# Gated delta net: the triangular inverse as two diagonal blocks of 64 per head, and sample attention with both groups in one item

## The chip, the core and the metric

One NeuronCore of one Trainium2 chip runs the whole program in one launch. The metric is device time in microseconds (us) of that launch; lower is better.

## What is computed

One decoder layer is evaluated for 1024 prompt rows and for 64 sample rows (8 sequences of 8 new tokens, each with a cache of 256). The layer reads one projection of the normalised input and runs three groups of heads on it (attention, gated delta net, S5), joins them in an output projection, and ends with an MLP. Two parts matter here. The delta net, cut from the reference:

```python
kb = kc * bc[..., None]
a_mat = jnp.where(strict, jnp.einsum('nbhid,nbhjd->nbhij', kb, kc) * decay, 0.0)
rhs = jnp.concatenate([vc * bc[..., None], kb * jnp.exp(gc)[..., None]], axis=-1)
sol = lax.linalg.triangular_solve(a_mat + eye, rhs, left_side=True, lower=True)
u, w = sol[..., :dv], sol[..., dv:]
def step(S, xs):
    v_new = u_i - jnp.einsum('bhck,bhkv->bhcv', w_i, S)
    o_i = (jnp.einsum('bhck,bhkv->bhcv', q_i * jnp.exp(g_i)[..., None], S)
           + jnp.einsum('bhij,bhjv->bhiv', aqk_i, v_new))
    S = (S * jnp.exp(g_last)[..., None, None] + ...)
```

And the sample rows' attention: three softmax branches (keys pooled in blocks of 64, the selected keys, a window), each over a sequence's cache and its own 8 new rows, added with gates `gt[..., 0:1] * o_c + gt[..., 1:2] * o_s + gt[..., 2:3] * o_w`. There are 8 query heads in 2 groups of 4; a group shares its keys and values.

## The kernel before

The stages run one after the other, each with its own instruction streams for the five engines (PE is TensorE, DVE VectorE, ACT ScalarE, POOL GpSimd, SP the DMA queue). Semaphores set the order between engines, and each engine runs its own list in order. The delta net stands between about 406 and 738 us of the span, sample attention between 738 and 821.

**Delta net.** The prompt is cut into 8 chunks of 128 rows (the reference's chunk of 64 is a choice; the result is the same), the sample rows are a ninth chunk of 64 (`TS`). `pairs()` takes them as (0,1), (2,3), (4,5), (6,7), (8). For each of four heads of a chunk the inverse T of the triangular matrix I + A is built by doubling, in `LEVELS` = 7 levels s = 0 to 6 (3 for the ninth chunk): at level s blocks of 2^s rows are joined to blocks of 2^(s+1). `AT` is A transposed, `TT` is T transposed. One level, for one chunk and four heads:

- POOL (L1253) masks: B = AT times the level's mask.
- PE (L1552) multiplies B by T (at level 0 by the identity); 4 matmuls of 128x128.
- ACT (L1321) copies the product out of PSUM to U.
- PE (L1562, L1563) multiplies T by U and U by TT; 8 matmuls (4 at the last level, which needs TT alone).
- DVE (L1408, L1410) subtracts both from T and TT.

Every matmul in float32 is two passes of PE, each with its weight load (PEld), so a 128x128 level of a pair of chunks is 48 passes. The two chunks of a pair alternate, so that one computes while the other's product is copied and subtracted.

Between the levels `after_level` puts steps that prepare the next pair's chunks, one step per level: first chunk a (levels 0 to 3), then chunk b (levels 4 to 6, its last step behind the first chunk's state update). Step 0 is `rows_of` (L1494: 6 transposes), whose result goes through ACT (squares), DVE and POOL (norm by a power, L1224; scaled keys and queries, L1230 and L1231) before step 1 can `turn` it (L1505: 8 transposes). Steps 2 and 3 make the matrices of the next A.

Behind level 6 stands the pair's tail: for each chunk the products with T (L1571, copied by ACT at L1327; L1613), the new values (copied by ACT at L1333), the output and the update of the state S.

**Sample attention.** Four items: two halves of four sequences, times the two groups. Scores of an item: for each of its four sequences five matmuls (L2177 to L2181: selected cache and new keys, window cache and new keys, pooled keys) with 64 rows and 32 weight columns. DVE adds the distances (L2298), reduces and scales (L2302 to L2317), ACT takes exponentials; PE turns the probabilities (L2190 to L2193: 7 transposes) and multiplies them by the values (L2205 to L2213: 19 matmuls, 64 weight columns). Items 0 to 3 have all their scores before the first turn.

## Time and profile before

| | us |
|---|---|
| median of 3 runs | 2117.62 (2117.27 to 2118.31) |
| profiled execution, its own time | 2112.89 |
| its span in the trace | 2110.7 |
| PE busy in the span | 1911.5 (91%) |
| DVE busy | 898.9 (43%) |
| ACT busy | 546.1 (26%) |
| POOL busy | 259.0 (12%) |

The page's shares are means over the whole span; most of PE's time is the output projection and the MLP. The two stages that the change touches take 416 of the 2110.7 us, so they are read by themselves, by stretches of the span. PEclk in such a view is the clock granted to TensorE, as a share of the full one.

### The profile page before, as it was taken

The numbers are of one execution on the slowest core, as the hardware profiler recorded it, in microseconds if no ns is written. First come the engines' busy times: TensorE is split into PE (matmuls) and PEld (weight loads), VectorE is DVE, ScalarE is ACT, GpSimd is POOL, SyncE is SP. The second block draws the span as 40 slices with busy tenths as digits, with TensorE's granted clock in tenths as the row PEclk, the third lists the DMA queues.
The fourth block names the chain that finished last, engine by engine and source line by source line (L and its number), as shares of the span: only waits on it lengthen the run. The fifth ranks groups of instructions, "written<-read, shape, count | busy, mean of one in ns | idle before, by whom it ended". The sixth has DMA issues, their size and how long they took to land. (4 is left out here: it accounts for less than half of the span.)

```text
span 2110.7 us, 26308 instructions
## 1 busy us (share of the span) xinstructions
PE 1911.5 (91%) x10850; PEld 1624.8 (77%) x10850; DVE 898.9 (43%) x1580; ACT 546.1 (26%) x994; POOL 259.0 (12%) x291
## 2 busy tenths in 40 slices
PE   2899989769998697999999898899999999999997
PEld 2898889768888575555555587899999999999996
DVE  4643351134444523454444353244444444444446
ACT  3122221212222114444443332211111211111212
POOL 0200000043344101000110000100000011111000
PEclk6899999879999665899999999999999999999999
DMA  4000022110000010000000301111111111111102
GB/s 117 22 31 22 23 72 104 54 56 1 1 1 26 12 59 25 1 1 1 20 21 0 125 1 40 41 40 60 40 41 41 41 60 41 41 41 41 41 30 85
DMA packets 31161, 80.03 MB, mean 38 GB/s; under 512 B 11183, under 2 KB 17279, under 8 KB 25763
## 3 DMA queue, kind: packets, MB, share of 16 engines
q1 hardware_dynamic: 30978, 78.27, 11.0%
q8 instruction: 86, 1.41, 0.3%
q14 instruction: 33, 0.26, 0.0%
q0 software_dynamic: 64, 0.09, 0.0%
HBM read 70.32 MB, written 10.12 MB: 38 GB/s over the span
## 5 line engine op out<-in xcount | busy, mean ns | idle before, releaser
L275 PE MATMUL ps<-mix_hi,wbuf 128*128 128x364 f32 (+1 forms) x768 | 254.1, 331 | 9.5 <-DVE wbuf L2659 6.1
L276 PE MATMUL ps<-mix_lo,wbuf 128*128 128x364 f32 (+1 forms) x768 | 253.6, 330 | 0.0
L277 PE MATMUL ps<-mix_hi,wbuf 128*128 128x364 f32 (+1 forms) x768 | 253.6, 330 | 0.0
L2695 DVE TENSOR_TENSOR x<-x,ps 128x512 f32<-128x512 f32 (+1 forms) x288 | 190.7, 684 | 120.2 <-PE ps L277 120.2
L275 PE MATMUL ps<-wbuf,mlp_hid_hi 128*128 128x512 f32 x576 | 225.3, 391 | 4.4 <-DVE wbuf L2659 4.4
L276 PE MATMUL ps<-wbuf,mlp_hid_hi 128*128 128x512 f32 x576 | 225.2, 391 | 0.0
L277 PE MATMUL ps<-wbuf,mlp_hid_lo 128*128 128x512 f32 x576 | 225.0, 391 | 0.0
L2681 DVE TENSOR_TENSOR mlp_hid_lo<-mlp_rect,mlp_hid_hi 128x364 fp32r<-128x364 f32 (+1 forms) x96 | 75.1, 783 | 290.0 <-ACT mlp_hid_hi L2602 290.0
L2653 POOL TENSOR_TENSOR mlp_rect<-mlp_rect 128x364 f32<-128x364 f32 (+1 forms) x96 | 76.0, 791 | 661.3 <-ACT mlp_rect L2624 661.3
L275 PEld LDWEIGHTS ps<-mix_hi,wbuf 128*128 128x128 f32 x768 | 146.3, 190 | 10.5 <-DVE wbuf L2659 6.4
L276 PEld LDWEIGHTS ps<-mix_lo,wbuf 128*128 128x128 f32 x768 | 145.8, 190 | 0.5
L277 PEld LDWEIGHTS ps<-mix_hi,wbuf 128*128 128x128 f32 x768 | 145.7, 190 | 0.0
L1893 PE MATMUL ps<-tokens,pa_vaug 128*65 128x512 f32 x264 | 141.3, 618 | 0.0
L1977 ACT ACTIVATE tokens<-ps 128x512 f32<-128x512 f32 (+1 forms) x148 | 88.0, 595 | 184.9 <-PE ps L1872 96.9
L275 PEld LDWEIGHTS ps<-wbuf,mlp_hid_hi 128*128 128x128 f32 x576 | 108.7, 189 | 27.0 <-DVE wbuf L2659 4.8
L277 PEld LDWEIGHTS ps<-wbuf,mlp_hid_lo 128*128 128x128 f32 x576 | 108.7, 189 | 22.7
L276 PEld LDWEIGHTS ps<-wbuf,mlp_hid_hi 128*128 128x128 f32 x576 | 108.7, 189 | 22.2
L2047 DVE TENSOR_REDUCE pa_mxp<-ps 128x1 f32<-128x512 f32 (+4 forms) x154 | 91.1, 617 | 75.2 <-PE ps L1847 49.2
L2624 ACT ACTIVATE mlp_rect<-ps 128x364 f32<-128x364 f32 (+1 forms) x96 | 45.4, 473 | 299.0 <-PE ps L277 299.0
L2596 ACT ACTIVATE wbuf<-mlp_raw_down 128x2048 fp32r<-128x2048 f32 x16 | 30.6, 1913 | 315.1 <-PE ps L277 315.1
L1841 PE MATMUL ps<-pa_Ka,pa_Q 128*128 128x512 f32 (+3 forms) x192 | 88.2, 520 | 21.9 <-DVE pa_part L2040 20.3
L1253 POOL TENSOR_TENSOR dn_B<-dn_AT,dn_level 128x512 f32<-128x512 f32 (+1 forms) x59 | 73.5, 1262 | 127.8 <-DVE dn_aqkT L1388 47.9
(532 smaller groups left out, 3724.2 us busy)
## 6 DMA issues: line engine op xcount, KB each, us to landing
out_raw<-in_w_up SPq DMA_DIRECT2D x16, 1024.0 KB, 4.8
mlp_raw_down<-in_w_down SPq DMA_DIRECT2D x16, 1024.0 KB, 4.8
feat_raw<-in_w_feat SPq DMA_DIRECT2D x12, 512.0 KB, 4.5
spare<-in_w_token SPq DMA_DIRECT2D x4, 1056.0 KB, 6.0
ln_x<-in_x_prompt SPq DMA_DIRECT2D x8, 512.0 KB, 4.1
ck<-in_cache_nsa SPq DMA_DIRECT2D x16, 256.0 KB, 3.0
out_raw<-in_w_out SPq DMA_DIRECT2D x4, 1024.0 KB, 4.7
x<-in_x_prompt SPq DMA_DIRECT2D x8, 512.0 KB, 6.2
```

The lines of the kernel that those rows point to most:

```text
L275: pe.matmul(out, lhs[0], rhs[0], start=first, stop=False)
L276: pe.matmul(out, lhs[0], rhs[1], start=False, stop=False)
L277: return pe.matmul(out, lhs[1], rhs[0], start=False, stop=last)
L1253: pool.tensor_tensor(B[:n, x, :, :n], AT[:n, k % 4, :, :n], mask, ALU.mult).then_inc(b_ready, 1)
L1841: last = pe.matmul(bank[:, x * w:(x + 1) * w], Q0[:, g, h * P:(h + 1) * P], Ka[:, br, g, k0:k0 + w], start=x == 0, **args)
L1893: pe.matmul(m.ps[:VW, 5 + br, :], v, PT[st % PTN][:k, :], start=first, stop=s == branch_end(n, br)).then_inc(pv_step, 1)
L1977: act.activation(PT[st % PTN][:rows, :], m.ps[:rows, 3 + x % 2, :], ACT.Exp).then_inc(ring_out, 1)
L2047: dve.tensor_reduce(mxp[:, heads[0]:heads[-1] + 1, col:col + 1], bank[:, 0:w * len(heads)].rearrange("p (h n) -> p h n", h=len(heads)), AX ...
L2624: act.activation(rect[:, (rank[u] - 1) % RT, :w], m.ps[:, u % 8, :w], ACT.Relu).then_inc(rectified, 1)
L2653: pool.tensor_tensor(part, part, part, ALU.mult).then_inc(squared, 1)
L2681: dve.tensor_tensor(hid[1][:, g % 2, a, o:o + w], rect[:, (rank[u] - 1) % RT, :w], hid[0][:, g % 2, a, o:o + w], ALU.subtract).then_inc(hi ...
L2695: dve.tensor_tensor(part, part, m.ps[:n, u % 8, :], ALU.add).then_inc(added, 1)
```

## The change

In the delta net the 64x64 diagonal blocks of T and TT are kept and doubled by themselves up to level 5 (`in_blocks`), with 64x64 matmuls that alternate between the upper and the lower half of the rows; `own` and `beside` are the two halves of columns of the same buffers, in which T and TT, or B's working part and the kept blocks of AT, lie side by side. ACT copies these blocks of AT out once per chunk (`at_kept`), and POOL's masks are 64 columns wide. Level 6 joins the blocks: it takes the corner of AT by itself, with no mask, and writes one corner of TT. DVE subtracts T and TT in one instruction. The other steps of a pair, and where they stand, are as before.

In sample attention an item is two sequences with both groups: `qS` holds a query's columns with zeros in the other group's rows, so a matmul runs over all 128 rows with 64 weight columns, and each sequence's own 8 new keys and 4 pooled keys lie behind its cache in `kT`. The values are multiplied with both groups' 128 weight columns at once, and half of the result is used. Eight small DMAs move the new values to where a matmul can read them. Each DVE step covers two branches in one instruction.

```diff
...
-    t["level"] = np.concatenate([((i >> s) == (p >> s) + 1) & (i >> (s + 1) == p >> (s + 1))
-                                 for s in range(LEVELS)], 1).astype(f)
+    ph, ih = p % 64, np.arange(64)[None, :]
+    t["level"] = np.concatenate([((ih >> s) == (ph >> s) + 1) & (ih >> (s + 1) == ph >> (s + 1))
+                                 for s in range(LEVELS - 1)], 1).astype(f)
+    t["eye64"] = (ph == ih).astype(f)
...
+        def in_blocks(k):
+
+            return SLEVELS if k == TS else LEVELS - 1
+
+        def order_b(k, s):
+
...
+        def blocks(k):
+
+            return [slice(0, BW)] + [slice(BW, P)] * (k < TS)
+
+        def own(t, k):
+            return t[:ROWS[k], k % 2, :, 0:BW]
+
+        def beside(t, k):
...
+                pool.memset(TT[:], 0.0).then_inc(s_zero, 1)
...
@@ -1241,16 +1255,19 @@
                 for p, pair in enumerate(pairs()):
                     for s in range(levels(pair[0])):
                         for k in pair:
+                            if s == in_blocks(k):
+                                continue
                             n, x = ROWS[k], k % 2
-                            pool.wait_ge(a_ready, 4 * (k + 1))
+                            if s == 0:
+                                pool.wait_ge(at_kept, k + 1)
                             if s:
                                 pool.wait_ge(bt, order(k, s - 1))
                             elif k >= 2:
                                 pool.wait_ge(bt, order(k - 2, LEVELS - 1))
                             if s == 1:
                                 pool.wait_ge(t_ready, order(k, 0))
-                            mask = C["level"][:n, s * P:s * P + n].unsqueeze(1).to_broadcast([n, H, n])
-                            pool.tensor_tensor(B[:n, x, :, :n], AT[:n, k % 4, :, :n], mask, ALU.mult).then_inc(b_ready, 1)
+                            mask = C["level"][:n, s * BW:s * BW + BW].unsqueeze(1).to_broadcast([n, H, BW])
+                            pool.tensor_tensor(own(B, k), beside(B, k), mask, ALU.mult).then_inc(b_ready, 1)
                         after_level(p, s, {1: scale})
...
@@ -1310,15 +1327,22 @@
                 for p, pair in enumerate(pairs()):
                     for s in range(levels(pair[0])):
                         for k in pair:
+                            n, x = ROWS[k], k % 2
                             if s == 0:
+                                act.wait_ge(a_ready, 4 * (k + 1))
+                                if k >= 2:
+                                    act.wait_ge(b_ready, order_b(k - 2, in_blocks(k - 2) - 1))
+                                for blk in blocks(k):
+                                    last = act.activation(B[blk, x, :, BW:P], AT[blk, k % 4, :, blk], ACT.Copy)
+                                last.then_inc(at_kept, 1)
                                 continue
-                            n, x = ROWS[k], k % 2
                             act.wait_ge(bt, order(k, s))
                             if s > 1:
                                 act.wait_ge(tut, order1(k, s - 1))
                             elif k >= 2:
...
-                            act.activation(U[:n, x, :, :n], heads(m.ps[:n, 3 * x, :])[:, :, :n], ACT.Copy).then_inc(u_ready, 1)
+                            rows = slice(0, n) if s < in_blocks(k) else slice(BW, P)
+                            act.activation(U[rows, x, :, 0:BW], heads(m.ps[rows, 3 * x, 0:H * BW]), ACT.Copy).then_inc(u_ready, 1)
...
@@ -1396,19 +1420,27 @@
                         for k in pair:
                             n, x = ROWS[k], k % 2
                             if s == 0:
-                                eye = m.ident[:n, :n].unsqueeze(1).to_broadcast([n, H, n])
-                                dve.wait_ge(b_ready, order(k, 0))
-                                link(dve.tensor_tensor(TT[:n, x, :, :n], eye, B[:n, x, :, :n], ALU.subtract))
+                                eye = C["eye64"][:n].unsqueeze(1).to_broadcast([n, H, BW])
+                                dve.wait_ge(b_ready, order_b(k, 0))
+                                link(dve.tensor_tensor(beside(T, k), eye, own(B, k), ALU.subtract))
                                 dve.wait_ge(bt, order(k, 0))
-                                dve.tensor_tensor(T[:n, x, :, :n], eye, heads(m.ps[:n, 3 * x, :])[:, :, :n],
-                                                  ALU.subtract).then_inc(t_ready, 1)
+                                dve.tensor_tensor(own(T, k), eye, heads(m.ps[:n, 3 * x, 0:H * BW]), ALU.subtract).then_inc(t_ready, 1)
                                 continue
                             dve.wait_ge(tut, order1(k, s))
-                            if s < levels(k) - 1:
-                                link(dve.tensor_tensor(T[:n, x, :, :n], T[:n, x, :, :n],
-                                                       heads(m.ps[:n, 3 * x + 1, :])[:, :, :n], ALU.subtract))
-                            dve.tensor_tensor(TT[:n, x, :, :n], TT[:n, x, :, :n],
-                                              heads(m.ps[:n, 3 * x + 2, :])[:, :, :n], ALU.subtract).then_inc(t_ready, 1)
+                            both = heads(m.ps[:n, 3 * x + 1, :])
+                            if k < 2 and s == in_blocks(k) - 1:
+                                dve.wait_ge(s_zero, 2)
+                            if s < in_blocks(k) - 1:
+                                dve.tensor_tensor(T[:n, x], T[:n, x], both, ALU.subtract).then_inc(t_ready, 1)
+                            elif s < in_blocks(k):
+                                if k < TS:
+                                    dve.tensor_tensor(T[0:BW, x, :, 0:BW], T[0:BW, x, :, 0:BW], both[0:BW, :, 0:BW], ALU.subtract)
+                                for blk in blocks(k):
+                                    last = dve.tensor_tensor(TT[blk, x, :, blk], T[blk, x, :, BW:P], both[blk, :, BW:P], ALU.subtract)
+                                last.then_inc(t_ready, 1)
+                            else:
+                                dve.tensor_scalar(TT[0:BW, x, :, BW:P], heads(m.ps[0:BW, 3 * x + 2, 0:H * BW]), -1.0, None,
+                                                  ALU.mult).then_inc(t_ready, 1)
...
@@ -1539,7 +1571,8 @@
                     for s in range(levels(pair[0])):
                         for k in pair:
                             n, x = ROWS[k], k % 2
-                            pe.wait_ge(b_ready, order(k, s))
+                            if s < in_blocks(k):
+                                pe.wait_ge(b_ready, order_b(k, s))
...
@@ -1549,8 +1582,13 @@
                                 pe.wait_ge(s_ready, k - 1)
                                 pe.wait_ge(w_ready, 2 * (k - 1))
                             for h in range(H):
-                                last = pe.matmul(m.ps[:n, 3 * x, h * P:h * P + n], B[:n, x, h, :n],
-                                                 T[:n, x, h, :n] if s else m.ident[:n, :n], start=True, stop=True)
+                                if s == in_blocks(k):
+                                    last = pe.matmul(m.ps[BW:P, 3 * x, h * BW:(h + 1) * BW], AT[0:BW, k % 4, h, BW:P], T[0:BW, x, h, 0:BW],
+                                                     start=True, stop=True)
+                                    continue
+                                for blk in blocks(k):
+                                    last = pe.matmul(m.ps[blk, 3 * x, h * BW:(h + 1) * BW], B[blk, x, h, 0:BW],
+                                                     T[blk, x, h, 0:BW] if s else m.ident[blk, blk], start=True, stop=True)
                             last.then_inc(bt, 1)
                         for k in pair:
                             if s == 0:
@@ -1558,9 +1596,17 @@
                             n, x = ROWS[k], k % 2
                             pe.wait_ge(u_ready, order1(k, s))
                             for h in range(H):
+                                if s == in_blocks(k):
+                                    last = pe.matmul(m.ps[0:BW, 3 * x + 2, h * BW:(h + 1) * BW], U[BW:P, x, h, 0:BW], TT[BW:P, x, h, BW:P],
+                                                     start=True, stop=True)
+                                    continue
                                 if s < levels(k) - 1:
-                                    pe.matmul(m.ps[:n, 3 * x + 1, h * P:h * P + n], TT[:n, x, h, :n], U[:n, x, h, :n], start=True, stop=True)
-                                last = pe.matmul(m.ps[:n, 3 * x + 2, h * P:h * P + n], U[:n, x, h, :n], TT[:n, x, h, :n], start=True, stop=True)
+                                    for blk in blocks(k):
+                                        pe.matmul(m.ps[blk, 3 * x + 1, h * P:h * P + BW], T[blk, x, h, BW:P], U[blk, x, h, 0:BW],
+                                                  start=True, stop=True)
+                                for blk in blocks(k):
+                                    last = pe.matmul(m.ps[blk, 3 * x + 1, h * P + BW:(h + 1) * P], U[blk, x, h, 0:BW], T[blk, x, h, BW:P],
+                                                     start=True, stop=True)
                             last.then_inc(tut, 1)
...
+                for b in range(NB):
+                    sp.dma_start(vnew[:, b], m.kv[b * NQ:(b + 1) * NQ, TS, VSEL:VSEL + 3 * P].rearrange("q (a n) -> q a n", a=3)[:, ::2, :]
+                                 ).then_inc(rows_moved, 16)
+
+            @block.gpsimd
+            def _(pool):
+                pool.memset(qS[:], 0.0).then_inc(q_zero, 1)
 
...
                 def scores(it):
-                    g, h = items[it]
-                    half = slice(64 * g, 64 * g + 64)
                     if it >= 2:
                         pe.wait_ge(sc_out, it - 1)
-                    sel, win, cmp = score_banks(it)
-                    for b in range(4):
-                        rows = slice(32 * b, 32 * b + 32)
-                        seq = 4 * h + b
-                        q = qS[half, seq].rearrange("p r q -> p (r q)")
-                        pe.matmul(sel[rows, 0:PAST], q, kT[half, 0, seq * PAST:(seq + 1) * PAST], start=True, stop=True)
-                        pe.matmul(sel[rows, PAST:], q, kselT[half, :], start=True, stop=True)
-                        pe.matmul(win[rows, 0:PAST], q, kT[half, 1, seq * PAST:(seq + 1) * PAST], start=True, stop=True)
-                        pe.matmul(win[rows, PAST:], q, kwinT[half, :], start=True, stop=True)
-                        last = pe.matmul(cmp[rows, :], q, kcT[half, :], start=True, stop=True)
+                    x = 2 * (it % 2)
+                    for i in range(2):
+                        rows = slice(64 * i, 64 * i + 64)
+                        b = 2 * it + i
+                        q = qS[:, b].rearrange("p g r q -> p (g r q)")
+                        pe.matmul(m.ps[rows, x, 0:KEYS + BLK], q, kT[:, b, SEL, :], start=True, stop=True)
+                        last = pe.matmul(m.ps[rows, x + 1, 0:KEYS], q, kT[:, b, WIN, 0:KEYS], start=True, stop=True)
                     last.then_inc(sc, 1)
 
                 def turn_probs(it):
@@ -2186,37 +2236,33 @@
                     pe.wait_ge(scaled, it + 1)
...
                 def values(it):
-                    g, h = items[it]
-                    half = slice(64 * g, 64 * g + 64)
                     pt = PT[:, it % 2]
                     pe.wait_ge(p_out, 3 * (it + 1))
                     if it >= 2:
                         pe.wait_ge(o_out, it - 1)
-                    acc = m.ps[half, 4 + it % 2, 0:P]
...
+                            pe.matmul(acc, ck[:, PAGES * b + a, 384:512], pt[:, a, rows], start=a == 0, stop=False)
+                            pe.matmul(acc, cw[:, PAGES * b + a, 128:256], pt[:, 2 + a, rows], start=False, stop=False)
+                        for c in (SEL, WIN):
+                            pe.matmul(acc, vnew[:, b, c, :], pt[:NQ, 4 + c, rows], start=False, stop=False)
+                        last = pe.matmul(acc, vcs[:, b, :], pt[:BLK, 6, rows], start=False, stop=True)
                     last.then_inc(pv, 1)
```

PE's order in the delta net, level 4 of a pair: `dn_B` is the masked matrix, `mixT` the next chunk's columns for `rows_of`, `dn_qk` the first input of `turn`; and the alternation of two lines, which repeats eight times, is shown once. First as it was before:

```order
L1552 MATMUL ps<-dn_T,dn_B 128x128 x8
L1562 MATMUL ps<-dn_U,dn_TT 128x128
L1563 MATMUL ps<-dn_TT,dn_U 128x128
L1494 MATMUL ps<-ident,mixT 128x128 x6
L1552 MATMUL ps<-dn_T,dn_B 128x128 x8
L1562 MATMUL ps<-dn_U,dn_TT 128x128
L1563 MATMUL ps<-dn_TT,dn_U 128x128
L1505 MATMUL ps<-ident,dn_qk 128x128 x4
```

And now, the same place:

```order
L1590 MATMUL ps<-dn_T,dn_B 64x64 x16
L1605 MATMUL ps<-dn_U,dn_T 64x64 x2
L1608 MATMUL ps<-dn_T,dn_U 64x64 x2
L1526 MATMUL ps<-ident,mixT 128x128 x6
L1590 MATMUL ps<-dn_T,dn_B 64x64 x16
L1605 MATMUL ps<-dn_U,dn_T 64x64 x2
L1608 MATMUL ps<-dn_T,dn_U 64x64 x2
L1537 MATMUL ps<-ident,dn_qk 128x128 x4
```

Every product stands where it stood, with twice as many matmuls of a quarter of the size, and the six transposes of `rows_of` and the first of `turn` stand between the same levels.

ACT's order at the end of a pair and the start of the next, before: `dn_wT` and `dn_vnew` belong to the tail of the old pair, `dn_sq` and `dn_qk` to the preparation of a later chunk, `dn_U` to level 1.

```order
L1327 ACTIVATE dn_wT<-ps 64x256 x2
L1333 ACTIVATE dn_vnew<-ps 128x256
L1327 ACTIVATE dn_wT<-ps 64x256 x2
L1333 ACTIVATE dn_vnew<-ps 128x256
L1283 ACTIVATE dn_sq<-ps 128x512
L1284 ACTIVATE dn_qk<-ps 128x512
L1321 ACTIVATE dn_U<-ps 128x512 x2
```

And now:

```order
L1351 ACTIVATE dn_wT<-ps 64x256 x2
L1357 ACTIVATE dn_vnew<-ps 128x256
L1351 ACTIVATE dn_wT<-ps 64x256 x2
L1357 ACTIVATE dn_vnew<-ps 128x256
L1336 ACTIVATE dn_B<-dn_AT 64x4x64 x4
L1300 ACTIVATE dn_sq<-ps 128x512
L1301 ACTIVATE dn_qk<-ps 128x512
L1345 ACTIVATE dn_U<-ps 128x4x64 x2
```

The copies of the kept blocks, four for the two chunks, stand between the last copy of the new values and the squares.

PE's order in sample attention, where the scores begin, before: `cw` is the window cache, turned by 16 transposes ahead of the scores.

```order
L2161 MATMUL ps<-ident,cw 128x128 x16
L2177 MATMUL ps<-sa_kT,sa_qS 32x256
L2178 MATMUL ps<-sa_kselT,sa_qS 32x64
L2179 MATMUL ps<-sa_kT,sa_qS 32x256
L2180 MATMUL ps<-sa_kwinT,sa_qS 32x64
L2181 MATMUL ps<-sa_kcT,sa_qS 32x32
```

And now:

```order
L2216 MATMUL ps<-ident,cw 128x128 x16
L2230 MATMUL ps<-sa_kT,sa_qS 64x268
L2231 MATMUL ps<-sa_kT,sa_qS 64x264
L2230 MATMUL ps<-sa_kT,sa_qS 64x268
L2231 MATMUL ps<-sa_kT,sa_qS 64x264
```

Twenty matmuls of an item became four.

## Rows read from the trace of the kernel before

**Rows 1.** Windows: length; busy us of PE, PEld, DVE, ACT, POOL; clock; DMA; GB/s.

```profile
446.00:692.00 246.00, 220.78 (x1800) 207.12 (x1800) 109.62 (x208) 62.57 (x142) 100.25 (x94) 0.99 0.02 6
692.00:738.00 46.00, 27.93 (x190) 24.14 (x189) 27.29 (x42) 5.03 (x14) 9.94 (x4) 0.65 0.06 13
738.00:822.00 84.00, 78.17 (x538) 60.54 (x539) 18.76 (x74) 17.42 (x63) 0.64 (x3) 0.60 0.12 37
```

**Rows 2.** The same view: levels of the pair of chunks 2 and 3.

```profile
517.28:529.03 11.75, 9.66 (x80) 8.84 (x80) 8.81 (x16) 2.94 (x6) 8.03 (x9) 1.00 0.00 1
529.03:550.67 21.64, 21.57 (x182) 20.89 (x183) 8.75 (x15) 5.21 (x12) 8.67 (x7) 1.00 0.01 1
550.67:559.20 8.53, 6.83 (x58) 6.26 (x56) 5.55 (x11) 3.32 (x7) 5.23 (x7) 1.00 0.01 3
559.20:566.24 7.04, 6.97 (x57) 6.54 (x57) 1.38 (x2) 2.18 (x6) 2.44 (x2) 1.00 0.00 0
566.24:578.40 12.16, 10.37 (x81) 9.41 (x81) 3.66 (x12) 2.43 (x7) 1.26 (x1) 1.00 0.00 1
```

**Rows 3.** Who waited for whom, 446 to 692: total us, times, longest.

```profile
ACT dn_U L1321 <- PE ps L1552: 57.5, 44, 5.2
PEld ps L1552 <- POOL dn_B L1253: 18.5, 22, 1.7
```

**Rows 4.** Timeline of chunk 4's preparation: start, length, engine, operation, count, idle before.

```profile
519.44 0.82 PE L1494 MATMUL ps<-ident,mixT 128*128 128x128 f32 x6
525.99 0.61 POOL L1231 TENSOR_TENSOR dn_qg<-dn_qk,dn_gate 128x256 f32<-128x256 f32 x1
527.29 0.60 PE L1505 MATMUL ps<-ident,dn_qk 128*128 128x128 f32 x4
```

**Rows 5.** Timeline of small tiles on PE and PEld (shapes: weights, then moving).

```profile
137.17 2.16 PE L996 MATMUL ps<-fs_x,mixT 128*64 128x8 f32 x64
152.23 3.71 PE L971 MATMUL ps<-fs_x,mixT 128*64 128x128 f32 x64
692.36 0.54 PEld L1552 LDWEIGHTS ps<-ident,dn_B 64*64 64x64 f32 x8
```

**Rows 6.** Timeline, tail of the first pair, and two rows of the sample chunk.

```profile
504.81 0.38 PE L1514 MATMUL ps<-dn_featT 64*128 64x128 f32 x2
505.12 1.16 PE L1571 MATMUL ps<-dn_TT,dn_kbg 128*128 128x128 f32 x8
506.31 0.78 ACT L1327 ACTIVATE dn_wT<-ps 64x256 f32<-64x256 f32 x2 [1.03 <-PE ps L1571]
694.31 0.71 POOL L1253 TENSOR_TENSOR dn_B<-dn_AT,dn_level 64x256 f32<-64x256 f32 x1 [15.57 <-DVE dn_T L1403]
702.68 1.78 PEld L1571 LDWEIGHTS ps<-dn_TT,dn_kbg 64*128 64x128 f32 x8 [0.69 <-DVE dn_TT L1410]
```

**Rows 7.** TensorE's busy time and granted clock in three stretches.

```profile
506.00:508.00 2.00, 1.13 (x11) 1.00 0.00 0
694.00:696.00 2.00, 0.92 (x8) 0.83 0.18 33
764.00:790.00 26.00, 26.00 (x135) 0.50 0.00 1
```

**Rows 8.** Sample attention: two stretches of PE, and four rows of VectorE.

```profile
761.33:790.52 29.19, 29.19 (x161) 0.54 0.00 1
790.52:820.98 30.46, 27.71 (x182) 0.50 0.00 1
767.61 1.01 DVE L2298 SCALAR_TENSOR_TENSOR sa_probs<-sa_dist,sa_slope,ps 128x320 f32<-128x320 f32 x2 [6.43 <-PE ps L2181]
768.81 0.97 DVE L2302 TENSOR_REDUCE sa_mx<-sa_probs 128x1 f32<-128x320 f32 x3
792.90 0.16 DVE L2310 TENSOR_SCALAR sa_rs<-sa_rs 128x3 f32<-128x3 f32 x1
794.39 0.16 DVE L2310 TENSOR_SCALAR sa_rs<-sa_rs 128x3 f32<-128x3 f32 x1
```

More of the change, by code:

```diff
@@ new lines, in score_banks @@
+            return m.ps[:, x:x + 2, 0:KEYS], m.ps[:, x, KEYS:KEYS + BLK]
+        (consts, weights, cw_loaded, rows_moved, sigmoids, q_zero, q_out, turned, pages_out, window_out, pooled, pool_out, gated, sc, sc_out,
+         nm_ready, exp_done, scaled, p_turned, p_out, pv, o_out, vec) = (sem(n) for n in (
+             "consts", "weights", "cw_loaded", "rows_moved", "sigmoids", "q_zero", "q_out", "turned", "pages_out", "window_out", "pooled",
+             "pool_out", "gated", "sc", "sc_out", "nm_ready", "exp_done", "scaled", "p_turned", "p_out", "pv", "o_out", "vec"))
@@ L2289, in _ @@
-                dve.wait_ge(pool_out, 8)
-                dve.wait_ge(consts, 64)
+                    dve.tensor_copy(kT[:, 2 * a:2 * a + 2, WIN, 0:PAST], m.ps[:, a, :].rearrange("p (b n) -> p b n", b=2)).then_inc(window_out, 1)
+                dve.wait_ge(gated, 1)
+                link(dve.tensor_reduce(gates[:], picked[:].rearrange("p i (h c) -> p i c h", c=3), AX.X, ALU.add))
                 def rows(it):
-                    g, h = items[it]
                     probs = probs_of[:, it]
+                    keys, blocks = score_banks(it)
@@ L2295, in rows @@
                     dve.wait_ge(sc, it + 1)
-                    for b, ((o, w), src) in enumerate(zip(BR, score_banks(it))):
-                        table = dist[:, h, :] if b < 2 else dcmp[:, h, :]
-                        last = dve.scalar_tensor_tensor(probs[:, o:o + w], table, slope[:, g:g + 1], src, ALU.mult, ALU.add)
-                    last.then_inc(sc_out, 1)
+                    dve.scalar_tensor_tensor(two(probs), dist[:, 0:KEYS].unsqueeze(1).to_broadcast([P, 2, KEYS]), slope[:, 0:1], keys,
+                                             ALU.mult, ALU.add)
@@ L2300, in rows @@
+                    dve.scalar_tensor_tensor(branch(probs, CMP), dist[:, KEYS:], slope[:, 0:1], blocks,
+                                             ALU.mult, ALU.add).then_inc(sc_out, 1)
                     dve.wait_ge(sc_out, it + 1)
-                    for b, (o, w) in enumerate(BR):
-                        last = dve.tensor_reduce(mx[:, it, b:b + 1], probs[:, o:o + w], AX.X, ALU.max)
-                    link(last)
+                    dve.tensor_reduce(mx[:, it, 0:2], two(probs), AX.X, ALU.max)
```

183 lines of the change are left out of this document (84 added, 99 removed).

## The prediction

> **What bounds the kernel now.** I read the views by stage first, since the page's shares average over stages. In the paired loop of the delta net (446 to 692) PE is busy 220.8 of 246 us, and the next engine, DVE, 110 [rows 1]: PE is the bound, and its granted clock there is .99, so its passes run at the upper level (2.4 GHz). In the two stretches behind it the clock is .65 and .60 [rows 1]: there PE spends much time at the lower one (1.2 GHz), and a pass costs more.
>
> One pair of chunks, level by level [rows 2]: levels 0 and 1 take 11.75 us, levels 2 to 4 21.64, level 5 8.53, level 6 7.04, the tail 12.16, in all 61.1. Levels 2 to 4 are PE without a gap (21.57 of 21.64 busy, 182 passes, .119 each). Levels 0 and 1, and level 5, are not: PE is busy 9.7 of 11.75 and 6.8 of 8.53. What they wait for shows in the view of waits: PE's loads wait 18.5 us for POOL's masks, 22 times [rows 3]. The longest name there, ACT waiting 57.5 us for PE's products, is an engine with time to spare. POOL's mask is late because the norm of the next chunk stands on POOL: from `rows_of` at 519.44 to the scaled queries, at 525.99 + .61, are 7.16 us, and `turn` (527.29) comes behind it [rows 4]. This chain of ACT, DVE and POOL is a floor for a stretch between `rows_of` and `turn`, whatever PE does.
>
> **The delta net's products.** A level of a pair had 48 passes of 128x128, 5.7 us at .119. It gets 96 of 64x64. No row has such passes on alternating tiles, so I bound them. The ninth chunk's 64x64 passes on one tile took .54 for 8, .067 each [rows 5]: the upper end, nothing overlapping. 64 passes that alternate between two column halves took 2.16, .034 each, and with 128 moving columns 3.71, .058, half of the loop's .119 [rows 5]: two tiles do run beside each other. I take .034, half of .067, as alternating is what the new code does. A level is then 3.3 us instead of 5.7.
>
> - Levels 2 to 4: 288 passes by .034 (9.8), the 38 other passes at .119 (4.5), .4 for waits and changes of tile: 14.7, so -6.9.
> - Levels 0 and 1: `rows_of` ends its wait at +1.25 (32 passes and its start), the chain's 7.16 makes 8.4; POOL's remaining work is 1.15 and its new mask .71 (the ninth chunk's mask had that size [rows 6]): level 2 starts at 10.3 instead of 11.75, -1.45. Without the chain it would be 5.
> - Level 5: chain-bound too, 7.16 less the .7 by which `rows_of` stands ahead, and .95 for eight transposes (.60 for four and overlap [rows 4]): 7.4 for 8.53, -1.1.
> - Level 6: 32 passes on single tiles by .067 (2.1), .7 for a copy that fewer passes cover, 24 others at .119: 5.7 for 7.04, -1.3.
> - Tail: the kept blocks add two ACT copies (.78 for two such sizes [rows 6]) and a POOL mask (.71) between ACT's last copy and level 0. The last products of the tail stand behind that copy as well and hide most: +.3, between 0 and 1.5.
>
> A change of tile size leaves a gap: the last passes with 64 rows begin at 504.81, two in some .2, and the next with 128 rows at 505.12 [rows 6], so about .1 us; it is in the sums. The Trainium skill ("TensorEngine Tiling (Array Packing)", Key Properties) says that a change of the tiling mode drains the engine, which speaks against the change; it gives no price.
>
> Together -10.45 a pair, -41.8 for four; the first pair has no tail to hide its .78 + .71, +1.5. DVE's single subtraction and the narrower masks lie beside PE. The ninth chunk keeps its 64 rows: nothing. **-40.3 at full clock.**
>
> **The clock.** This is the part that I price last and trust least. The clock stayed at full in a tail where PE was busy only 1.13 of 2 us, with tiles of 128 rows [rows 7]. It fell (.83 in the stretch) at 694 to 696, where PE had been on 64x64 tiles and then waited 2.04 us for POOL; and it was .50 through 764 to 790, where PE never idled but worked with 64 rows [rows 7, 8]. So tiles of 64 rows hold the clock less well. The new loop has tiles of 64 rows in each block, two together, and a wait of over 2 us before each of seven `turn`s. At the lower clock a pass of 128 columns goes from .119 to .222 (1.78 for 8 [rows 6]), nearly double. I expect the clock to fall at the waits, and the dense levels, with both halves of the array at work, to bring it back. Where it returns I can't read; I take half a level's extra behind chunk a's `turn` (1.8; a level at half costs 3.3 more), three quarters behind chunk b's (2.5, the small join follows), and a tail entered low costs its 10.37 us of PE [rows 2] almost again: 9.0 by .222/.119, 10.4 doubled, I take 9.7. Four times 1.8, three times 2.5 and two of four tails: 7.2 + 7.5 + 19.4 = **+34.1**, between 0 and far more (below). The delta net comes to -6.2.
>
> **Sample attention.** Scores end the wait at 761.33 and reach the first `turn_probs` at 790.52, 29.2 us of unbroken PE at a clock of .54 [rows 8]. Now an item has 8 passes of 264 or 268 columns with all 128 rows: at .119 for 128 columns .25 each, 2.0 us. DVE's two fused steps on 528 columns instead of 640 (1.01 and .97 [rows 8]: .83 and .8), the pooled keys' .24, the maximum's .17 and starts make 2.3 an item, so DVE is the bound. Three items and the first scaling (792.90 to 794.39, 1.5 [rows 8]) come before the first turn: 761.3 + .4 + 2.0 + 3 x 2.3 + 1.5 = 772.1, 18.4 earlier. Behind it 2.3 + 1.5 = 3.8 to the second turn; three turns of 7 passes (4.7) and 112 passes of values, whose weight loads have 128 columns, at the lower clock's .222 (24.9); .8 for the last copies: 806.3 against 820.98, **-14.7**. I keep the lower clock, which the old stretch had throughout [rows 8]; at the full one it would be up to 12 us less. The eight small DMAs and the copies stand ahead of the wait at 761 and are needed after the turn: nothing; if one were late by its own length, a few us.
>
> **The sum.** -40.3 + 34.1 - 14.7 = -20.9 on the profiled execution's 2112.89 (span 2110.7), 2092.0. That execution lies 4.7 below the runs' median, 2117.62, so the median goes to **2097**. By itself this case runs from 2080 (one tail low) to 2112 (three and a half).
>
> **The rivals.**
> - A, the clock never falls: -40.3 - 14.7 = -55, 2063. For it: the old loop held .99 with pauses. Against it: rows 7. Chance .15.
> - B, all four tails low: another 19.4, 2116, no change to be measured. Chance .13.
> - C, the clock stays low through the loop, slower than before. Levels 0 and 1 +.5; levels 2 to 4 288 x .068 + 38 x .238 + .4 = 29.0, +7.4; level 5 +.6; level 6 +3.7; tail +10: +22 a pair, +89, and +1.5 - 14.7: 2194. It is decided by whether dense levels of alternating 64x64 tiles bring the clock back; if they don't, nothing does. For it 764 to 790, unbroken and low; against it that both halves work here at once. Chance .10.
> - D, the blocks don't overlap, .067 a pass: levels 0 and 1 -.4, levels 2 to 4 24.2 (+2.6), the rest as above: about 0 a pair, then +1.5 - 14.7, 2105 at full clock. The rows of .034 speak against it. Chance .07. The Trainium skill ("TensorE: Matmul & The Clock Gate", Back-to-back issue gap) names about 62 ns per matmul instruction as a floor where hardware decode is off; by it 288 passes would take 17.9 us and the sum at full clock would come to about 2099. The row of .034 disagrees.
>
> The main case has .50, other mixtures .05. **How the numbers follow.** About .2% (4 us) is what a measurement here can tell from no change. Faster: A .15, most of the main case .44, D .06, other .03: .68. Same: parts of B and the main case's upper end: .12. Slower: C .10, B's and the main case's far ends .10: .20. Ends cut to 2 in 10 outside: the low end takes in A, 2060; the high end B with some more clock lost, 2130; C lies outside.
>
> **What would show it.** Levels 2 to 4 near 15 us a pair at clock 1.00 and L1590 to L1608 near .034 a pass: the product step; .067 is D. A stretch of levels 0 and 1 near 10 us: the chain's floor. The clock in the four tails, and in 2 us stretches behind each turn: the +34. A first turn of probabilities some 18 us earlier after the scores' start, and 34 us from there to the end: the sample part. I am wrong if the clock behaves otherwise than a fall at the waits and a return in the dense levels, or if POOL's mask, not PE, ends every level.

## The result and the profile after

The changed kernel takes **2068.94 us** (median of 4 runs, 2065.6 to 2072.31) against 2117.44 beside it: ratio 0.977, 95% interval 0.975 to 0.979, some 48 us less. I forecast 2097, in a range of 2060 to 2130: the sign was right, the size less than half.

The profiled execution (2070.01, span 2068.1) is read first by the same stages as before. A profile shows one execution: in some experiments below (e3, e7, e8, e10) it is 4 to 11 us below the median of its kernel, so what its stretches gain need not be what the median gains. Views of stretches of the changed kernel; columns as in [rows 1]: length, busy us of PE, PEld, DVE, ACT and POOL with their instructions, granted clock, DMA share, GB/s. They are the paired loop, the ninth chunk, the preparation of sample attention (turns of pages and window, pooled keys), the scores up to the first turn of probabilities, and the rest up to the prompt attention.

```profile
461.40:662.10 200.70, 165.44 (x2786) 150.85 (x2786) 77.40 (x183) 54.88 (x150) 62.02 (x83) 0.93 0.03 8
662.10:708.60 46.50, 26.24 (x190) 22.74 (x189) 26.88 (x40) 5.30 (x15) 10.32 (x5) 0.73 0.06 14
708.60:738.20 29.60, 26.43 (x187) 25.82 (x186) 4.95 (x14) 5.46 (x9) 0.14 (x1) 0.62 0.31 90
738.20:747.20 9.00, 5.62 (x32) 3.19 (x32) 6.57 (x23) 4.12 (x18) 0.00 (x0) 0.82 0.01 2
747.20:782.40 35.20, 32.13 (x141) 29.15 (x141) 5.51 (x23) 7.13 (x27) 0.06 (x1) 0.51 0.00 0
```

The same preparation in the kernel before (PE alone, clock, DMA share, GB/s):

```profile
738.70:761.30 22.60, 20.55 (x194) 0.83 0.43 136
```

From starts of instructions that stand in both traces:

| stretch, us | before | changed | difference | forecast |
|---|---|---|---|---|
| first transposes of the delta net to the first pair | 35.6 | 34.6 | -1.0 | +1.5 |
| four pairs | 237.3 | 200.8 | -36.5 | -41.8 + 34.1 |
| ninth chunk, output turns | 46.7 | 46.5 | -.3 | 0 |
| preparation of sample attention | 22.3 | 29.5 | +7.3 | 0 |
| scores to the first turn | 29.2 | 9.1 | -20.1 | -18.4 |
| from there to the prompt attention | 30.8 | 35.1 | +4.4 | +3.7 |
| the rest of the kernel | 1289.4 | 1285.7 | -3.7 | 0 |
| sum | | | -49.9 | -20.9 |

The stretches read here differ by more than the spans (42.6), because what stands ahead of the delta net took 7.3 longer in this execution. It has the same code and still moves from one execution to the next (its end, the first transposes, lies at 419.4 in the profile of before and between 420.9 and 426.7 in those of the changed kernel and the experiments), and the rest of the kernel by some 3 us. So I read each stretch by itself.

Where the loop's time went shows by levels. The pair of chunks 2 and 3 again, beside [rows 2]: levels 0 and 1, 2 to 4, 5, 6, the tail; and below them two stretches of it, behind the first and the second `turn`:

```profile
515.90:526.30 10.40, 6.56 (x143) 1.00 0.01 2
526.30:542.10 15.80, 15.75 (x326) 0.89 0.01 4
542.10:549.20 7.10, 4.21 (x105) 1.00 0.01 2
549.20:557.90 8.70, 8.14 (x59) 0.61 0.00 0
557.90:570.20 12.30, 10.51 (x83) 1.00 0.01 2
526.50:529.90 3.40, 3.40 (x68) 0.52 0.02 7
550.40:557.20 6.80, 6.25 (x35) 0.51 0.00 0
```

Lengths are 10.4, 15.8, 7.1, 8.7 and 12.3; at full clock I had 10.3, 14.7, 7.4, 5.7 and 12.5. The clock falls where I said, behind the waits, for 3.4 us in the first case and 6.8 in the second; levels 2 to 4 and level 6 are 1.1 and 3.0 longer than I had at full clock. The tail is untouched (1.00). Rows of PE in that pair:

```profile
542.12 1.15 PE L1590 MATMUL ps<-dn_T,dn_B 64*64 64x64 f32 x32
543.81 0.28 PE L1608 MATMUL ps<-dn_T,dn_U 64*64 64x64 f32 x4
543.93 0.28 PE L1605 MATMUL ps<-dn_U,dn_T 64*64 64x64 f32 x4
548.25 0.63 PE L1537 MATMUL ps<-ident,dn_qk 128*128 128x128 f32 x4 [2.52 <-issue]
550.95 1.96 PE L1600 MATMUL ps<-dn_TT,dn_U 64*64 64x64 f32 x16 [0.56 <-ACT dn_U L1345]
557.87 1.16 PE L1617 MATMUL ps<-dn_TT,dn_kbg 128*128 128x128 f32 x8
```

32 passes in 1.15 are .036 each, where I took .034. Both figures hold the length of the last pass too; by their starts, four alternating passes come every .12 us (L1608, then L1605), some .03 each. `turn` (L1537) waits 2.52 for the chain; behind it the join's 16 passes (L1600) take 1.96, where 1.14 is the time at full clock (the same passes in e3, below); the tail's first products take the 1.16 that they took before [rows 6].

### The profile page after: what moved, and what is told of

Its sections match the earlier page's. It is cut to its first block and busy times, and to the rows that moved or that the text cites. A ratio compares the mean times of both kernels' runs of the same rounds, so it can differ in the third digit from the quotient of the medians.

```text
span 2068.1 us, 27935 instructions
## 1 busy us (share of the span) xinstructions
PE 1850.6 (89%) x11698; PEld 1576.6 (76%) x11698; DVE 866.3 (42%) x1540; ACT 541.1 (26%) x1001; POOL 223.7 (11%) x285
## 5 line engine op out<-in xcount | busy, mean ns | idle before, releaser
L266 PEld LDWEIGHTS ps<-wbuf,mlp_hid_hi 128*128 128x128 f32 x576 | 108.7, 189 | 26.9 <-DVE wbuf L2703 4.8
L1887 PE MATMUL ps<-pa_Ka,pa_Q 128*128 128x512 f32 (+3 forms) x192 | 88.5, 523 | 22.7 <-DVE pa_part L2086 21.2
L266 PE MATMUL ps<-kvp_whi,h_hi 128*128 128x264 f32 x288 | 82.7, 287 | 5.3 <-DVE kvp_wlo L346 5.3
```

The costliest lines, as they stand in the source:

```text
L266: pe.matmul(out, lhs[0], rhs[0], start=first, stop=False)
L1887: last = pe.matmul(bank[:, x * w:(x + 1) * w], Q0[:, g, h * P:(h + 1) * P], Ka[:, br, g, k0:k0 + w], start=x == 0, **args)
```

## The experiments

**e1 and e2, each half alone.**

```diff
e1, against the changed kernel:
-                        pe.matmul(m.ps[rows, x, 0:KEYS + BLK], q, kT[:, b, SEL, :], start=True, stop=True)
+                        pe.matmul(sel[rows, 0:PAST], q, kT[half, 0, seq * PAST:(seq + 1) * PAST], start=True, stop=True)
...

e2, against the changed kernel:
-                                for blk in blocks(k):
-                                    last = pe.matmul(m.ps[blk, 3 * x, h * BW:(h + 1) * BW], B[blk, x, h, 0:BW],
...
+                                last = pe.matmul(m.ps[:n, 3 * x, h * P:h * P + n], B[:n, x, h, :n],
...
```

> The delta net of the changed kernel with the sample attention of the kernel before. Theory F (the clock falls only for some microseconds behind the turns, and no tail of a pair is run at the lower level): the stretch from the first rows_of to the ninth chunk's first product, 272.9 us before and 235.4 in the changed kernel, is 235 again, and the whole about 37 below before, 2080. Rival P (the prediction's term: the clock takes back 34 of 40): 2111, with tails of pairs at half clock.

> The sample attention of the changed kernel with the delta net of before. In the changed kernel's profile the scores took 20 us less, the values 4 more, and the preparation ahead of the scores (page and window turns, pooled keys) 7.3 more, most of it at the lower clock. Theory F: those 7.3 are where the clock happened to return and not of the change, so the preparation takes about 23 here and the whole is 16 below before, 2101. Rival G: the preparation's new shapes keep the clock low, it takes about 30, and the whole is 9 below, 2109.

Measured: e1 2086.41 (2075.2 to 2087.51; ratio 0.983, 0.980 to 0.986), e2 2100.03 (0.991, 0.990 to 0.993), against 2119.26. In stretches, e1's loop and its preparation (before's code), then e2's preparation (the changed code) and the rest of its sample attention from the first turn:

```profile
456.20:659.10 202.90, 167.10 (x2788) 0.92 0.03 8
705.40:734.90 29.50, 27.43 (x194) 0.61 0.33 104
```

```profile
742.30:765.00 22.70, 19.63 (x186) 0.82 0.41 117
773.10:808.30 35.20, 32.12 (x140) 0.51 0.00 0
```

The delta net's gain is there by itself: 202.9 for the pairs, near the 200.8 above and far from the 230 that my clock term asked for. The preparation is the surprise. Before's code takes 29.5 us behind the new delta net (clock .61), and the changed code 22.7 behind the old one (.82). So rival G is out: the 7.3 us are not of the new shapes. They also explain why e1 lies 6 us above its expected 2080.

**e3, the waits filled.**

```diff
                 def turn(k):
                     n, x = ROWS[k], k % 2
+                    if k > 1:
+                        for _ in range(10):
+                            pe.matmul(m.ps[:, 2, 0:P], m.ident[:], m.ident[:], start=True, stop=True)
                     pe.wait_ge(normed, k + 1)
```

> The changed kernel with ten 128x128 products, whose result nobody reads, on TensorE ahead of each turn of the paired loop, where it waits some 2.5 us for the norm. Theory F (the wait is what lets the clock fall): clock 1.00 through the loop, levels 2 to 4 14.7 instead of 15.8, level 6 5.7 instead of 8.6 where it was low; some 1 us for each of four first chunks and 3 for two second ones: 9 to 11 below the changed kernel, about 2059. Rival W (tiles of 64 rows let it fall whatever stands in the wait): clock as before and 2069. Rival P (the clock cost 34): 2035.

Measured 2063.42 (2052.66 to 2066.15; 0.974, 0.972 to 0.976, against 2119.26), some 5 us below the changed kernel, with intervals that just touch. The trace, which is of the fastest of its five executions (2052.66), is clearer: the loop, its first 5.8 us alone, the five stretches of the second pair, and the join's second product in that pair:

```profile
459.00:651.20 192.20, 173.14 (x2928) 0.99 0.03 9
458.80:464.60 5.80, 4.32 (x51) 0.50 0.01 3
511.60:522.00 10.40, 8.97 (x165) 1.00 0.01 3
522.00:536.50 14.50, 14.46 (x328) 1.00 0.01 3
536.50:543.60 7.10, 6.63 (x126) 1.00 0.01 2
543.60:549.40 5.80, 5.23 (x57) 1.00 0.01 3
549.40:561.80 12.40, 10.60 (x83) 1.00 0.00 1
545.30 1.14 PE L1603 MATMUL ps<-dn_TT,dn_U 64*64 64x64 f32 x16 [0.57 <-ACT dn_U L1345]
```

The clock is 1.00 throughout but for the first 5.8 us, where the loop still runs at the lower level that it came in with; the loop takes 192.2 instead of 200.8. So filling the waits takes 8.6 us off this loop, not 34, and what lets the clock fall in this loop is the wait: the same 64x64 tiles keep it at full once 2.5 us of 128x128 work stand in front of `turn`. The changed loop didn't begin low, so turn by turn, by the starts of the same products in both traces, its clock cost a little more: .8 to 1.4 behind each of four first turns and 2.5 and 2.8 behind two of three second ones, 10.1 in all, of which e3's own low start hides 1.5. Rivals W and P fall. The full-clock stretches are 10.4, 14.5, 7.1, 5.8 and 12.4 (forecast 10.3, 14.7, 7.4, 5.7, 12.5).

**e4, what brings the clock back ahead of a tail.** In PE's list (ACT's and DVE's follow):

```diff
-                if s - 4 in stages and b is not None:
+                if s - 4 in stages and s - 4 != 2 and b is not None:
...
                         last.then_inc(wprod, 1)
+                        if k % 2 and second_of(p) is not None:
+                            odd_grams(second_of(p))
...
                         if k % 2 == 0 and second_of(p) is not None:
-                            odd_grams(second_of(p))
+                            even_grams(second_of(p))
```

> The changed kernel with the second chunk's even grams (16 + 8 passes of 128 columns) moved from behind level 6 to behind the first chunk's state update, and its odd grams behind the second chunk's first product; nothing is left out. Theory F (dense products with 128 rows bring the clock back): the first chunk's tail follows level 6's small tiles directly and is run at the lower level, 4 to 5 us more in each of two or three pairs, less .9 of filled wait a pair: 6 to 12 above the changed kernel, about 2078. Rival T (the clock comes back by itself after about 7 us): no tail slower, 2067 to 2069.

Measured 2060.83 (0.972, 0.971 to 0.974): below the changed kernel, so the expected total was wrong. The tails did what F said. The first chunk's tail with the moved grams (the products of keys and queries for the next A), of the second pair, where the clock hadn't fallen, and of the third, where it had; PE from the third pair's `turn` up to its grams, and from there on; and the first products (L1621) of the third pair's two chunks:

```profile
550.80:559.30 8.50, 7.60 (x61) 1.00 0.00 0
601.70:613.70 12.00, 11.13 (x61) 0.63 0.01 1
596.90:610.50 13.60, 12.73 (x75) 0.50 0.00 1
610.50:613.70 3.20, 3.20 (x26) 0.99 0.00 0
```

```profile
601.53 2.07 PE L1621 MATMUL ps<-dn_TT,dn_kbg 128*128 128x128 f32 x8
613.54 1.16 PE L1621 MATMUL ps<-dn_TT,dn_kbg 128*128 128x128 f32 x8
```

The third pair's first tail takes 12.0 at .63 instead of 8.5; its products 2.07, and the second chunk's, behind the grams, 1.16. So without the grams between them a tail does follow at the lower clock. That they stood there before the tail is what I had overlooked. In the changed kernel the clock is back at 557.1, in the last of the grams, .8 before the tail. That the grams themselves bring it back isn't shown: in e4 the lower clock lasted through 13.6 us, the tail's own products among them, and was back as the grams began (610.5). It did not return after some 7 us by itself, so T is out. The loop as a whole is 202.6 (200.8): filled waits (the .87 ahead of L1665 is gone in second chunks) pay most of it. The total is lower mainly because in this kernel the clock returned in the preparation's page turns (the transposes of the cache's pages): 23.6 instead of 29.5.

**e5, the changed kernel again.**

> The changed kernel once more, for the spread of its own clock from one execution to the next. Theory F: the same loop product by product; where the clock falls differs (the profile of the changed kernel lost 6.8 us behind two second chunks' turns, e1 with the same delta net behind another two), and the preparation of sample attention takes 22 to 24 us in some executions, 29.5 in others. Median 2066 to 2071. Rival G: 29.5 belongs to the change, and every profile of it shows it.

Measured 2068.60 (0.977, 0.975 to 0.979). Its profile repeats the first one: pairs 54.6, 54.2, 51.5 and 40.5, preparation 29.55, the clock falling at the same places, and so does the loop of e7. The other pattern (56.6 to 56.8, 51.5, 54.2 and 40.6, in all 2 us more) is that of e1, e9 and e11, which have the same loop in other programs. A spread between executions of one kernel, which I expected, doesn't show in its two profiles. It may still be there: both profiled executions had a mean granted clock of .938, the six others of these two runs .923 to .928, and their stretches aren't known. In the profiles the 7.3 us come with the new delta net ahead (e1) and not with the new sample attention (e2).

**e6, blocks one behind the other.**

```diff
...
-                                for blk in blocks(k):
+                            for blk in blocks(k) if s < in_blocks(k) else []:
+                                for h in range(H):
...
```

> The changed kernel with the passes of one block of all heads ahead of those of the other, instead of alternating by head. Theory O (the .036 a pass comes from neighbours on different tiles that run at the same time): consecutive passes share a tile, .06 to .067 each, levels 2 to 4 near 24 instead of 15 to 16, the loop 32 to 38 above the changed kernel, 2103. Rival S (a small pass is short wherever it stands): no change, 2069.

Measured 2102.04 (0.993, 0.991 to 0.995): 33 us given back by order alone, as theory O had it. The loop (457.0 on), levels 2 to 4 of the third pair, and the last pair:

```profile
457.00:700.30 243.30, 223.85 (x2787) 0.81 0.02 7
588.80:612.00 23.20, 23.20 (x324) 0.78 0.01 1
647.20:695.00 47.80, 45.15 (x485) 0.50 0.01 2
```

Levels 2 to 4 take 23.2 (14.5 in e3), all of it busy, and the clock is lower as well (.81 over the loop). The loop gives back more than the total, 42.5, since the preparation takes 23.7 here. More than half of that is the last pair, 62.8 instead of 40.5: it runs at the lower clock for 47.8 us although PE is busy for 45.2 of them. So the order costs twice, by the pass and by the clock. Two neighbours of level 1 in the third pair, two passes each, still at full clock:

```profile
582.58 0.28 PE L1608 MATMUL ps<-dn_T,dn_U 64*64 64x64 f32 x2
582.70 0.28 PE L1606 MATMUL ps<-dn_U,dn_T 64*64 64x64 f32 x2
```

They start .12 apart, a pass every .058 to .06, where the changed kernel starts four passes in the same .12. The Trainium skill ("TensorEngine Tiling (Array Packing)", Key Properties) says that tiles work independently and may load and multiply in parallel; the trace agrees where neighbours in the order stand on different tiles, two passes every .058 instead of one.

**e7, the first two turns of probabilities filled.**

```diff
+                    for _ in range((12, 7, 0, 0)[it]):
+                        pe.matmul(m.ps[:, 4, 0:P], m.ident[:], m.ident[:], start=True, stop=True)
                     pe.wait_ge(scaled, it + 1)
```

> The changed kernel with 12 and 7 products of 128x128, whose result nobody reads, ahead of the first and second turn of the probabilities, where TensorE waits 3.0 and 2.2 us. Theory V (the two waits let the clock fall, and it stays down through the values, 35.1 us from the first turn to the end): clock full there, about 12 less, 2057. Rival R (the values' own products do it, since three of seven have 8 or 4 rows only): the clock falls a few us later and the values gain 1 to 3, 2067.

Measured 2068.70 (0.977, 0.975 to 0.979): nothing that the runs can tell. In the trace, which is of the fastest execution (2062.89), the stretch from the first turn is 31.3 instead of 35.1, full clock up to 751.6 and then the lower one:

```profile
743.80:751.60 7.80, 7.17 (x59) 0.98 0.01 2
751.60:775.00 23.40, 22.60 (x98) 0.50 0.00 0
```

The clock falls although PE is busy 22.6 of 23.4 us, so it isn't the wait alone, and V is out. R stands, though not shown: three of seven value products have 8 or 4 rows, and they cost as much as those with 128 (two passes each; one pass has a median of .416 against .421 in the changed kernel, a weight load .328 against .333). The Trainium skill ("TensorE: Matmul & The Clock Gate", LDWEIGHTS) says that a load is paid by its columns, not its rows; the trace agrees, .328 with 8 or 4 rows for .333 with 128.

**e8, all of these waits filled, and e10, POOL's masks ahead of two scalings.** e8 adds to e3 and e7, with `m.ps[:, 7, 0:P]` and `m.ps[:, 3, 0:P]` as targets:

```diff
+                            if k == TS and s == 1:
+                                for _ in range(7):
...
+                            for _ in range(20):
...
                             pe.wait_ge(masked, 1)
...
+                    for _ in range({0: 10, TS: 18}.get(k, 0)):
...
                     pe.wait_ge(fin, 1 if k < TS else 2)
```

```diff
e10, against e8:
-                        after_level(p, s, {1: scale})
+                        after_level(p, s, {1: scale, 2: scale_rest})
```

> e3 and e7 together, and such products also in the ninth chunk's waits (7, 20) and ahead of the two groups of output turns (10, 18). Theory F: the loop 192 as in e3 (200.8 in the changed kernel); the ninth chunk 46 to about 41, as its 64-row products are at full clock for longer; the preparation always near 22; with theory V the values 23, else 33. 2040 to 2052. Rival: the added products delay what stands behind them, or the clock falls on the ninth chunk's own small tiles, and nothing is gained over e3, 2060 to 2063.

> e8 with the last two scalings of the next first chunk (two POOL instructions of .61) put behind the masks of level 2 instead of ahead of them. If POOL's queue behind the norm sets the start of level 2, as the prediction's sum of 10.3 had it (8.4 to the turn, 1.15 of POOL's other work, .71 of mask), level 2 follows the turn by .2 to .4 instead of 1.1 (.7 of it idle), .5 to .7 less in each of four pairs, the loop 189.5 to 190 instead of 192.2, 2047. Rival: the masks come earlier but level 2 waits for the turn's own end or for DVE's subtraction, 192, 2049.

e8: 2049.47 (2043.11 to 2058.71; 0.969, 0.965 to 0.973), about 19 below the changed kernel and below both kernels by more than any interval. Loop, ninth chunk, preparation, and from the first turn:

```profile
458.10:650.30 192.20, 173.20 (x2928) 0.99 0.03 9
650.30:695.20 44.90, 36.43 (x299) 0.89 0.07 14
695.30:717.80 22.50, 19.33 (x186) 0.83 0.40 118
725.90:757.30 31.40, 29.98 (x155) 0.62 0.00 1
```

In the profiled execution (2045.01) 8.6 us come from the loop, 7.0 from the preparation, 3.7 from the values, 1.5 from the ninth chunk, where I had expected 5. e10: 2053.24 (0.969, 0.967 to 0.971), not to be told from e8; in the trace its loop is 190.0 against 192.2. Level 2 of the second pair, e8 first and then e10:

```profile
520.10 0.38 PE L1540 MATMUL ps<-ident,dn_qg 128*128 128x128 f32 x2
521.19 1.37 PE L1596 MATMUL ps<-dn_T,dn_B 64*64 64x64 f32 x32 [0.71 <-POOL dn_B L1270]
```

```profile
519.76 0.38 PE L1546 MATMUL ps<-ident,dn_qg 128*128 128x128 f32 x2
520.07 1.15 PE L1602 MATMUL ps<-dn_T,dn_B 64*64 64x64 f32 x32
```

The .71 of waiting for POOL is gone, and the level follows the turn: POOL's queue behind the norm did set the start of level 2.

**e9 and e11, the preparation.** e9 is e8's last two lines alone. e11:

```diff
                     last.then_inc(turned, 1)
+                for _ in range(16):
+                    pe.matmul(m.ps[:, 5, 0:P], m.ident[:], m.ident[:], start=True, stop=True)
                 pe.wait_ge(weights, 32)
```

> The changed kernel with 10 and 18 products of 128x128, whose result nobody reads, ahead of the first and the last of the output turns of the delta net, where TensorE waits 2.7 and 4.9 us; the loop is as it was. Theory F (the preparation's 29.5 us are of the place at which the clock meets it, not of its shapes): the engine comes to the page turns with a clock that returns during them, and the preparation takes 22 to 24 as in e2, e3 and e8; loop 200.8, about 2062. Rival H (what counts is the loop ahead, which had its own falls): 29.5 stays, 2068.

> The changed kernel with 16 products of 128x128, whose result nobody reads, right behind the 16 page turns at the start of sample attention's preparation; e9 had shown that products ahead of the output turns don't bring that stage its clock. Theory F (unbroken products with 128 rows and 128 moving columns bring the clock back, those with 4 moving columns or 4 weight columns behind them don't): the clock returns during the 16, which take 4 to 7 us, and the rest of the preparation, 26 us in the changed kernel, takes 18 to 19 as in e2 and e3; in all 26 to 28.5 instead of 29.5, the low stretch from the page turns under 12 us instead of 23. Rival (the pooled products hold or lose the clock whatever stands ahead): 34 to 36.

e9: 2069.18 (0.976, 0.974 to 0.977), preparation 29.8. The output turns now have full clock, but two waits are left behind them (1.71 and 2.55 us of idle PE), the clock falls in them, and the preparation begins low as before: my remedy failed. e11: 2068.58 (2 runs; 0.976, 0.973 to 0.979), preparation 26.9. Page turns with the added products, and what follows; below, what follows the page turns in the changed kernel, in all and up to where its clock returns:

```profile
708.10:716.30 8.20, 8.20 (x50) 0.65 0.82 232
716.30:735.00 18.70, 15.56 (x170) 0.89 0.14 42
```

```profile
712.10:738.20 26.10, 22.93 (x171) 0.63 0.28 88
712.10:731.10 19.00, 19.00 (x131) 0.50 0.38 121
```

The clock returns during the added products, and the same work behind them takes 18.7 instead of 26.1. So here it rose in dense work with 128 columns. Without them the pooled products (4 moving or 4 weight columns) ran on at the lower clock for 19 us, although PE never idled. In some kernels (e2, e3, e4, e6, e8) the clock returns in or right behind the 16 page turns (3.5 us), in others (e1, e5, e9) it doesn't. Why the same 16 go with a return in one case and not in another stays open; the kernels differ in when the turns start.

## Why the prediction was wrong

- **The passes: right.** .034 for an alternating pass (.036 measured), .067 for the join (16 in 1.14, .071), each with the last pass's length in it, and each stretch of a pair at full clock within .3 us of its forecast (e3). Full-clock sum for four pairs: -41.8 forecast, -45.1 measured (237.3 to 192.2, with e3's low start of 1.5 still in it). The difference is in the last pair, which prepares no second chunk and so has no chain in its level 5: it fell from 52.8 to 39.2, 13.7 where I counted 10.45 for each pair alike.
- **The chain's floor: right.** Levels 0 and 1 came to 10.4 with 6.6 of PE's work; e10 moves it by POOL's queue alone.
- **The clock: the step that failed.** "Four times 1.8, three times 2.5 and two of four tails: 7.2 + 7.5 + 19.4 = +34.1" measured 10.1 in the loop (8.6 against e3). Where it falls (behind the waits at the turns) and that it returns in the dense alternating levels was right; so C is out. The first `turn` cost .8 to 1.4 instead of 1.8, the second 2.5 and 2.8 in two of three pairs, near the 2.5. The step that failed is the path into the tails, 19.4 of the 34.1. They cost nothing: not two of four, none. Between a second chunk's `turn` and the tail stand 24 gram passes with 128 columns, which I had left out; the clock was back in the last of them, and e4 shows that a tail without them is run low. With no tail low the forecast's own sum is 2078. (Its 2080 for one low tail is a slip: 2097 less 9.7 is 2087.)
- **A clock cost that I had put at nothing.** "Nothing" for the preparation of sample attention measured +7.3: before's code has it too behind the new delta net (e1). What sets it is open. Had the loop's 8.6 and these 7.3 stood for the 34.1, the sum would have been -39 instead of -20.9. Most of what is left to -49.9 is the last pair (3.2), the first stretch (-1.0 where I had +1.5) and the rest of the kernel (3.7), which the change doesn't touch.
- **Scores and values: right.** -20.1 for -18.4, with the scores' clock at .82; +4.4 for +3.7 at the lower clock, of which filled waits give back only some 4 us (e7).
- **The rivals.** The truth lies between the main case and A (2063), which I gave .15. D is what e6 builds: 2102, where I had 2105 with a clock at full; there the lower clock took a large part of the loss, so that agreement is partly luck. The waits that took the place of PE's work (`turn`, 2.5 us each) are real, and were in the forecast.

## What to carry to other kernels

Price small-tile work by its order: two 64x64 blocks are cheap only while neighbours in the list stand on different tiles (two passes every .058 against one; 33 us here, the clock's share included). When a change takes work from a bound engine, look at where its new waits stand and what comes next: here a wait of 2.5 us was followed by 3.4 us of lower clock where dense alternating levels came next, and by 6.8 where a small join and dense 128-wide products did. So list what stands between a wait and a later stage before you price that stage as low. A cheap filler in such waits (e8) made the kernel some 19 us faster than the change alone, and a stage that wasn't changed can win or lose by the clock that it meets.

## What I had not expected of the hardware

The low stretches are reproducible: three profiles of the same loop (the changed kernel, e5, e7) had the same four pairs to .02 us, though the time ahead of them differed by 4 us, and three others shared a second pattern. And the preparation took either 22.3 to 23.7 us (before, e2, e3, e4, e6, e8, e10) or 29.5 to 29.8 (the changed kernel, e1, e5, e7, e9), and nothing between, except where products were added in it (e11).
